# Latents' attention: projection in halves, two merge gates before its end, ten expert rows later

## The reference

```python
u = x * (1 + sc1) + sh1
xc, bg, cg, q, k, v, g_conv, g_na = jnp.split(u @ w_in, IN_SPLITS, axis=-1)
y_conv = short_conv(xc, bg, cg, conv_w)            # bg * conv3(cg * xc)
y_na = neighbourhood_attention(q, k, v, k_ctx, v_ctx, rpb)   # context tokens: plain attention
merged = (jax.nn.sigmoid(g_conv) * (y_conv @ w_conv_out) +
          jax.nn.sigmoid(g_na) * (y_na @ w_na_out))
x = layer_norm(ALPHA * x + ga1 * (merged @ w_o), ln1_g, ln1_b)
u2 = x * (1 + sc2) + sh2
x = layer_norm(ALPHA * x + ga2 * peer(u2, w_query, sub_keys, expert_u, expert_v), ln2_g, ln2_b)
```

## Time and profile before

| | us |
|---|---|
| median of 3 runs | 1879.93 (1879.83 to 1882.43) |
| the profiled execution | 1884.2 |
| its span, first to last instruction | 1882.4 |
| latents' attention on PE | 311.5 to 460.9 |
| latents' merge on PE | 460.9 to 630.3 |
| latents' norms, queries | 630 to 823 |
| stream of all experts | 823 to 1724 |

### The profile page before, as it was taken

How to read it: one execution, slowest core, us unless ns; L and a number is a source line. 1 busy time by engine, 2 the same in 40 slices (tenths; PEclk the granted TensorE clock), 3 DMA queues, 4 the chain that set the end, 5 groups by cost and what they waited for, 6 DMA issues and landing times.

```text
span 1882.4 us, 21570 instructions
## 1 busy us (share of the span) xinstructions
PE 1774.0 (94%) x8020; PEld 1143.8 (61%) x8020; DVE 1268.7 (67%) x2592; ACT 296.0 (16%) x665; POOL 894.2 (48%) x839
## 2 busy tenths in 40 slices
PE   5988999898999999998999999998889999999995
PEld 3675844454444359997888888886554434444442
DVE  1212568898589699988889768888865523236767
ACT  0120012554100011111100100106630000000000
POOL 1000336666455324253555645677865564435540
PEclk9998999999999999999999999999999999999998
DMA  9998779899999887589999999998999999999995
GB/s 395 396 344 314 266 206 391 307 333 324 365 364 389 346 291 284 179 320 372 363 407 393 391 347 407 409 406 322 353 349 409 409 409 409 409 409 409 409 410 227
DMA packets 171209, 670.22 MB, mean 356 GB/s; under 512 B 19771, under 2 KB 20923, under 8 KB 166365
## 3 DMA queue, kind: packets, MB, share of 16 engines
q0 software_dynamic: 112512, 410.26, 57.4%
q1 hardware_dynamic: 53840, 242.77, 33.0%
q10 hardware_dynamic: 4752, 15.81, 2.2%
HBM read 659.27 MB, written 7.39 MB: 354 GB/s over the span
## 4 chain that ended last, share of the span: by engine, by line
PE 65%; DVE 14%; DMA 10%; POOL 5%; issue 5%; ACT 1%; SPq 1%; ACTq 0%; DVEq 0%; POOLq 0%
PE psum L954 23%; PE psum L1028 16%; PE psum L1127 7%; DVE psum L1889 5%; POOL arena L612 5%; DMA arena<-in_expert_v_dram,arena 4%; PE psum L811 3%; DMA arena<-in_expert_u_dram,arena 3%; PE psum L786 2%; PE psum L1052 2%; PE psum L1055 2%; PE psum L981 2%; PE psum L1089 2%; PE psum L1115 1%; DMA arena<-in_w_ada_dram 1%
## 5 line engine op out<-in xcount | busy, mean ns | idle before, releaser
L612 POOL DMA_INDIRECT arena<-in_expert_u_dram,arena x384 | 468.5, 1220 | 354.1 <-DVE arena L1600 232.8
L1600 DVE CUSTOM_DVE_ANT_0 arena<-arena 128x1024 f32<-128x1024 f32 x384 | 459.5, 1222 | 167.3 <-DMA arena<-in_expert_u_dram,arena 154.5
L612 POOL DMA_INDIRECT arena<-in_expert_v_dram,arena x384 | 379.5, 988 | 360.2 <-DVE psum L1889 207.3
L1889 DVE SCALAR_TENSOR_TENSOR psum<-arena,psum 128x1024 f32<-128x1024 f32 x254 | 327.1, 1288 | 189.7 <-DMA arena<-in_expert_v_dram,arena 176.4
L954 PE MATMUL psum<-arena 128*128 128x256 f32 x2048 | 444.7, 380 | 6.6 <-DMA arena<-in_expert_uT_dram 6.6
L1028 PE MATMUL psum<-arena 128*128 128x512 f32 x1024 | 442.9, 594 | 0.4 <-DMA arena<-in_expert_v_dram 0.4
L954 PEld LDWEIGHTS psum<-arena 128*128 128x128 f32 x2048 | 390.6, 191 | 59.8 <-issue 7.0
L1028 PEld LDWEIGHTS psum<-arena 128*128 128x128 f32 x1024 | 193.7, 190 | 249.9 <-issue 249.6
L1127 PE MATMUL psum<-arena 128*128 128x128 f32 x1280 | 146.2, 275 | 1.4 <-DVE arena L1760 1.4
L1127 PEld LDWEIGHTS psum<-arena 128*128 128x128 f32 x1280 | 144.4, 192 | 3.3 <-issue 1.7
L1394 ACT ACTIVATE arena<-psum 128x512 f32<-128x512 f32 x64 | 38.2, 597 | 399.1 <-PE psum L954 399.1
(11 more groups left out here) (195 smaller groups left out, 1402.5 us busy)
## 6 DMA issues: line engine op xcount, KB each, us to landing
arena<-in_expert_uT_dram SPq DMA_DIRECT2D x128, 512.0 KB, 6.8
arena<-in_expert_v_dram SPq DMA_DIRECT2D x128, 512.0 KB, 6.8
arena<-in_w_ada_dram SPq DMA_DIRECT2D x12, 2048.0 KB, 16.5
arena<-in_w_in_dram SPq DMA_DIRECT2D x11, 2048.0 KB, 13.6
arena<-in_w_query_dram SPq DMA_DIRECT2D x8, 2048.0 KB, 12.7
arena<-in_w_in_dram SPq DMA_DIRECT2D x30, 512.0 KB, 7.4
arena<-in_w_o_dram SPq DMA_DIRECT2D x16, 512.0 KB, 5.3
arena<-in_expert_u_dram,arena POOLq DMA_INDIRECT x384, 8.9
```

The lines of the kernel that those rows point to most:

```text
L612: pool.indirect_dma_start(slot, None, table[0], bass.IndirectOffsetOnAxis(ap=number, axis=0)).then_inc(land, 16)
L1600: dve.tensor_tensor_reduce(UR[b], UR[b], U2B[e], 1.0, 0.0, ALU.mult, ALU.add, DOTS[e % 2][:, k:k + 1]).then_inc(u_free, 1)
L1889: dve.scalar_tensor_tensor(ys, row, weight, ys, ALU.mult, ALU.add).then_inc(v_free, 1)
```

## The change

It has five parts.

1. The pieces are cut into halves of 4 matmuls (`project_half`), and `HALVES` gives each pair from 0 to 13 one or two of them. A piece is opened by its first half (which waits for the copy of the piece ahead) and signalled by its second. Where a pair's two halves belong to two pieces (pairs 2, 3, 7 and 11) the second half there waits for ACT's copy of the piece that the first half has just ended; ACT's copy still stands at the end of its iteration (`PIECE_AFTER` now lists which pieces are copied in it).
2. The convolution gate of merge step 8 goes in two halves into pairs 14 and 15 (bank 5), that of step 9 stands whole between the last transposes and the last value product (bank 0). Merge steps 8 and 9 skip them; the sigmoid of step 8 becomes two instructions.
3. The convolutions move from behind the rows of pairs 2, 6, 10 to between the windows and the first row of pairs 3, 7, 11; the fourth stands behind the last pair.
4. Pair rows go from 70 to 60, the first two merge steps from 8 and 8 to 13 and 13.
5. The five parameter broadcasts move from the start of ACT's merge to behind its third sigmoid.

```diff
--- before.py
+++ after.py
@@ -113,8 +113,11 @@
 WHOLE, CONV_IN = (5, 3, 4), (0, 2, 1)
 PROJ_AT = tuple(range(6)) + tuple(6 + 4 * n for n in range(4))
 PROJ_CTX, PROJ_QKV = 6, PROJ_AT[-1]
-PIECE_AFTER = {0: 1, 1: 2, 2: 3, 4: 4, 5: 5, 6: 6, 8: 7, 9: 8, 10: 9, 12: 10, 13: 11}
-CONV_AFTER = {2: 0, 6: 1, 10: 2, 14: 3}
+HALVES = (2, 1, 2, 2, 1, 2, 1, 2, 1, 2, 1, 2, 1, 2)
+HALVES_TO = [2 + sum(HALVES[:i]) for i in range(len(HALVES) + 1)]
+PIECE_AFTER = {i: [m for m in range(1, 12) if HALVES_TO[i] <= 2 * m + 1 < HALVES_TO[i + 1]] for i in range(len(HALVES))}
+CONV_AFTER = {3: 0, 7: 1, 11: 2}
+GATE_HALVES, GATE_NEXT = {14: 0, 15: 1}, 16
 CONV_OPS = 5
 
 
@@ -801,15 +804,33 @@
                                            start=k == 0, stop=k == KD - 1)
                     mm.then_inc(proj_done, 1)
 
-            def project_piece(m):
-
+            def project_half(n):
+
+                m, half = divmod(n, 2)
                 c, i = divmod(m, len(CONV_IN))
-                weights(pe, ("conv", 1, c))
                 own = W_PARTS[slot_of["conv", 1, c]][:, i, :].rearrange("p (k n) -> p k n", n=P)
-                pe.wait_ge(proj_out, PROJ_QKV + m)
+                if half == 0:
+                    weights(pe, ("conv", 1, c))
+                    pe.wait_ge(proj_out, PROJ_QKV + m)
+                for k in range(4 * half, 4 * half + 4):
+                    mm = pe.matmul(bank(5), own[:, k, :], UT[:, k, CTX:NT], start=k == 0, stop=k == KD - 1)
+                if half == 1:
+                    mm.then_inc(proj_done, 1)
+
+            def first_gate(half):
+
+                wc = merge_weights(pe, "gconv", 1, 0, 0)
+                if half == 0:
+                    pe.wait_ge(proj_out, PROJ_QKV + 12)
+                for k in range(4 * half, 4 * half + 4):
+                    pe.matmul(bank(5), wc[:, k, :], UT[:, k, CTX:NT], start=k == 0, stop=k == KD - 1)
+
+            def second_gate():
+
+                wc = merge_weights(pe, "gconv", 1, 0, 1)
+                pe.wait_ge(win_step, NU - 2)
                 for k in range(KD):
-                    mm = pe.matmul(bank(5), own[:, k, :], UT[:, k, CTX:NT], start=k == 0, stop=k == KD - 1)
-                mm.then_inc(proj_done, 1)
+                    pe.matmul(bank(0), wc[:, k, :], UT[:, k, CTX:NT], start=k == 0, stop=k == KD - 1)
 
             pe.wait_ge(silu_step, 3)
             pe.wait_ge(cond_in, 48)
@@ -925,7 +946,8 @@
                 pe.wait_ge(po_out, 2)
 
             def latent_attention():
-                project_piece(0)
+                project_half(0)
+                project_half(1)
                 for i, n in enumerate(range(2, NU + 4, 2)):
                     if n < NU:
                         scores_of_pair(n)
@@ -934,8 +956,13 @@
                         turn(n - 1)
                     if n >= 6:
                         mix_of_pair(n - 4)
-                    if i in PIECE_AFTER:
-                        project_piece(PIECE_AFTER[i])
+                    if i < len(HALVES):
+                        for half in range(HALVES_TO[i], HALVES_TO[i + 1]):
+                            project_half(half)
+                    if i in GATE_HALVES:
+                        first_gate(GATE_HALVES[i])
+                    if i == GATE_NEXT:
+                        second_gate()
                 pe.wait_ge(po_out, outputs_upto(NU - 1))
 
             def expert_scores(m):
@@ -1047,9 +1074,10 @@
                         d = 8 * s + 4 * hf + c
                         if d >= 1:
                             pe.wait_ge(sig_out, d)
-                        wc = merge_weights(pe, "gconv", s, hf, c)
-                        for k in range(KD):
-                            pe.matmul(bank(0)[:, 0:n_tok], wc[:, k, :], UT[:, k, tok], start=k == 0, stop=k == KD - 1)
+                        if d not in (8, 9):
+                            wc = merge_weights(pe, "gconv", s, hf, c)
+                            for k in range(KD):
+                                pe.matmul(bank(0)[:, 0:n_tok], wc[:, k, :], UT[:, k, tok], start=k == 0, stop=k == KD - 1)
                         wn = merge_weights(pe, "gna", s, hf, c)
                         for k in range(KD):
                             mm = pe.matmul(bank(1)[:, 0:n_tok], wn[:, k, :], UT[:, k, tok], start=k == 0,
@@ -1290,8 +1318,8 @@
                         normalise(n + 1)
                     if n >= 6:
                         take_out(n - 3)
-                    if i in PIECE_AFTER:
-                        take_piece(PIECE_AFTER[i])
+                    for m in PIECE_AFTER.get(i, ()):
+                        take_piece(m)
 
             def normalise(n):
                 act.wait_ge(recip_done, n + 1)
@@ -1303,26 +1331,34 @@
 
             def load_x(e):
                 act.dma_start(XB[min(e, 1)], rows(x_prompt, x_sample, e)).then_inc(xb_in, 16)
+
+            def load_rows(s):
+
+                own = mods_d[s:s + 1, :]
+                for n, row in ((0, own[:, 2 * D:3 * D]), (1, ln1_g[0:1, :]), (2, ln1_b[0:1, :]),
+                               (3, own[:, 4 * D:5 * D]), (4, own[:, 3 * D:4 * D])):
+                    act.dma_start(PRM[s][n], row.partition_broadcast(P)).then_inc(prm_in[s], 16)
 
             def section(s):
                 t0, n_tok = SECTIONS[s]
                 if s == 0:
                     act.wait_ge(mods_out, 16)
-                else:
-                    act.wait_ge(win_step, NU - 2)
-                own = mods_d[s:s + 1, :]
-                for n, row in ((0, own[:, 2 * D:3 * D]), (1, ln1_g[0:1, :]), (2, ln1_b[0:1, :]),
-                               (3, own[:, 4 * D:5 * D]), (4, own[:, 3 * D:4 * D])):
-                    act.dma_start(PRM[s][n], row.partition_broadcast(P)).then_inc(prm_in[s], 16)
+                    load_rows(s)
                 for i in range(8):
                     d = 8 * s + i
                     act.wait_ge(gates_done, d + 1)
                     if d >= 1:
                         act.wait_ge(merge_step, 2 * d)
-                    src = bank(0, 2).rearrange("p (a b) -> p a b", a=2)[:, :, 0:n_tok]
-                    act.activation(SG[s], src, ACT.Sigmoid).then_inc(sig_out, 1)
+                    if d == 8:
+                        act.activation(SG[s][:, 0, :], bank(5), ACT.Sigmoid)
+                        act.activation(SG[s][:, 1, :], bank(1), ACT.Sigmoid).then_inc(sig_out, 1)
+                    else:
+                        src = bank(0, 2).rearrange("p (a b) -> p a b", a=2)[:, :, 0:n_tok]
+                        act.activation(SG[s], src, ACT.Sigmoid).then_inc(sig_out, 1)
                     if s == 1 and i == WEIGH_STEP:
                         weigh(0)
+                    if s == 1 and i == ROWS_STEP:
+                        load_rows(s)
                 if s == 0:
                     act.wait_ge(cache_out, 32)
                 load_x(s)
@@ -1615,13 +1651,14 @@
                     window(n)
                     window(n + 1)
                     rows = PAIR_ROWS[i]
+                    if i in CONV_AFTER:
+                        convolve_piece(CONV_AFTER[i])
                     context_rows(min(rows, 1))
                     normalise(n)
                     context_rows(min(rows - 1, 1))
                     normalise(n + 1)
-                    context_rows(rows - 2)
-                    if i in CONV_AFTER:
-                        convolve_piece(CONV_AFTER[i])
+                    context_rows(max(rows - 2, 0))
+                convolve_piece(3)
                 context_rows(BEFORE_MERGE)
 
             def route(e, part):
@@ -2046,9 +2083,10 @@
 PACE = NKEYS - RING - 9 - PACED_FROM
 assert (HK - BESIDE) % (2 * GROUP) == 0 and BESIDE % (2 * GROUP) == 0 and GATE_ROUNDS % 4 == 0
 FIRST_ROWS = 30
-PAIR_ROWS = (6, 6, 4, 2, 6, 6, 4, 2, 6, 6, 4, 2, 6, 6, 2, 2)
+PAIR_ROWS = (6, 3, 5, 3, 3, 6, 3, 3, 3, 6, 3, 3, 3, 6, 3, 1)
 BEFORE_MERGE = 12
-MERGE_ROWS, NORM_ROWS = (8, 8, 14, 14, 14, 14, 12, 3), 4
+MERGE_ROWS, NORM_ROWS = (13, 13, 14, 14, 14, 14, 12, 3), 4
+ROWS_STEP = 2
 WEIGH_STEP = 1
 CHOICE_ROWS = (5, 5, 5, 5, 4, 4, 4, 3, 3, 3)
 assert sum(MERGE_ROWS[:WEIGH_STEP + 1]) + BEFORE_MERGE + FIRST_ROWS + sum(PAIR_ROWS) == HK and len(CHOICE_ROWS) == 4 + PARTS
```

## The result

| | before | changed |
|---|---|---|
| median of 4 runs each | 1881.18 us | 1906.33 us |
| ratio, 95% interval | | 1.0133 (1.0107 to 1.0159) |
| span of the profiled execution | 1882.4 us | 1903.1 us |
| mean granted clock | 0.983 | 0.976 |

The change made the kernel 25 us slower; the interval of the ratio leaves out 1. I had forecast 10 slower, 1890.1 us, with a range up to 1901. The direction was right, the size was not. Ratios are of undisturbed executions only: one execution of the later kernel E7 took 6580.39 us and is left out, so E7 rests on three.

A forecast was written before the change was run, and what follows sets the result against it. TensorE was taken as the bound, with DVE setting the merge from step 10 on. Terms 6.6 + 1.4 - 1.0 + 3.2 gave +10.2 us, from a median of 1879.93 to 1890.1; range 1878 to 1901.

The forecast's parts named there:

- two signs of being wrong: Split waits under 1 us, or DVE entering merge step 10 before 523, would show the prediction wrong.
- A: Latents' attention up to the last transposes: +6.6 us, from about 0 to +10.
- C: First branch product to DVE's entry into merge step 10: 47.3 us, -1.0 against before.
- A, the old waits go: Latents' attention: TensorE's old waits vanish, -15.7 us, and the slow clock after the first long one, -2.7.
- A, pair 2: Pair 2 of the attention: +2.8 us waiting at the transposes, +1.4 at the split between two pieces.
- A, the split waits: Pairs 3, 7 and 11: second half waits 4.0 us for ACT's copy of the piece, three times, +12.0.
- A, the clock: Behind the three split waits: the clock falls after one in three, costing +1.7 us.
- B: Last transposes to first branch product: +1.4 us (-1.1 to +3.5), the branch weights' load replacing the gate taken out.
- D: Merge step 10 to output projection: +3.2 us, half of the five parameter broadcasts' 6.4 us of transfers.
- The rows in the attention are free: Latents' attention: the ten moved rows cost nothing there, since DVE would have had them hidden.
- the split is covered: Rival: pairs 2, 3, 7 and 11, copy done when the first half ends; A -8.5, sum -4.9, 1875 us; chance 0.10.
- Everything collides: Rival: three clock falls, late branch weights, slow rows, full broadcast cost: +10, +3.5, +4, +6.4, up to 1904; 0.13 above 1897.

The follow-up runs named there:

- E7: Changed kernel with ACT's piece copy ahead of the normalisations, ten rows back in the pairs and the second gate behind the last value product; 0.9910 of the kernel before.
- E1: Changed kernel, but in pairs 2, 3, 7 and 11 ACT copies value product and finished piece ahead of the two normalisations; 1.0040 of the kernel before.
- E3: Changed kernel with the ten rows back in the pairs (70 there, 8 and 8 in the first two merge steps); 1.0088 of the kernel before.
- E4: Changed kernel with the five parameter broadcasts back at the start of ACT's merge; 1.0118 of the kernel before.
- E6: Changed kernel with the second gate behind the last value product instead of ahead of it; 1.0069 of the kernel before.
- E9: Changed kernel, but POOL requests each gathered row of the first two tiles singly instead of in groups of four; 1.0104 of the kernel before.
- E12: E8 run once more, the same kernel; 0.9917 of the kernel before.
- E8: E7 with the five parameter broadcasts asked for at merge step 8 instead of step 10; 0.9896 of the kernel before.
- E2: Changed kernel, but in pairs 3, 7 and 11 DVE's convolution stands behind the pair's rows; 1.0032 of the kernel before.
- E11: Changed kernel with the halves undone, whole pieces where they stood before; 1.0109 of the kernel before.
- E10: E8 with four value rows moved from merge steps 10 to 13 to the normalisations behind the output projection; 0.9934 of the kernel before.

## Why the prediction was right and wrong, step by step

The mechanism was right in its parts: every wait that it named is in the trace, and neither of its two signs of being wrong appeared (the split waits are 3.97 us, DVE enters step 10 at 542.09). Two terms of the sum were sized wrongly, the clock in A and the rows in C, each with a clock price missing or too small.

- **What bounds the kernel**: right. TensorE is the chain up to step 10, and what is late there comes out at the end nearly one to one (E1: 16.7 us at the projection, 1.0133 to 1.0040, which is 17.5 us).
- **A, the old waits go**: right, -15.7 and -2.7 of clock. None of the waits of before is left.
- **A, pair 2**: 2.8 and 1.4 were forecast for transposes and split; measured are 1.28 + 0.55 and 0.78, and 1.6 of slow clock (0.4 on the transposes themselves, 1.2 on the products behind), which I had not listed. 4.2 forecast, 4.2 measured: that the sums agree is luck, with the waits put too high and a fall of the clock left out.
- **A, the split waits**: 4.0 us three times forecast, 3.97 measured, for the cause named.
- **A, the clock: the step that failed.** The prediction took one fall in three at 1.7 us, +1.7. It was three in three at 2.7 to 2.9, +8.3. Both factors were wrong. A wait of 4.0 lay between those of 1.2, which had left the clock alone (rows 4 don't show them; the row below does), and those of 4.76 and 5.05, and nothing in the trace of before told on which side. In the changed kernel and in E3, E4, E6 and E9 all 15 split waits, of 3.97 to 4.27 us, were followed by a fall. For the price I had used the average clock of a stretch behind the last transposes, where products are few. Here a half of a piece stood behind the wait, and its 3.67 us grew by three quarters. The same rows showed such a price, in the 2.7 us lost behind 346.72. The Trainium skill's rule, which the prediction quoted from TensorE: Matmul & The Clock Gate, "HAM oscillation — how this bites in real kernels", has the falls right: every round with such a wait was throttled anew. I gave that 0.05, and should have let it be the forecast.
- **B**: +2.2 for +1.4. Request at 10.5 us as worked out, landing 11.2 instead of 10.5. That a gate placed ahead of the last outputs gains nothing, because the load takes its place, was right, and E6 shows the place where it does gain.
- **C, the second step that failed**: 47.3 forecast, 54.7 measured. Of the 7.4, 2.7 are the clock behind the wait for the branch weights (the product took 6.26 instead of 3.60), which I had not charged although the wait was in my own sum. The other 4.7 are the rows: I had 37.5 us for 26 rows, of which 30.8 are 24 transfers at 409 GB/s and some 3 the way to the first request; for the remaining 3.7 the prediction gives no source. The 30.8 take the queues to be full from the first request on. From 500.83 to 515 they moved 261 GB/s instead, while the first requests came 2.29 us apart. At 409 GB/s what was not moved in these 14.17 us is worth 5.1 us, an estimate from these two rates. That the slow requests are the whole reason is argued and not shown.
- **D**: +1.3 for +3.2. Once DVE enters step 10 on time it is +4.4 (E3), and with the broadcasts in step 8 it is 1.7 to 3.2 less than with them in step 10 (E7 against E12 and E8). That the late entry hid the term in the changed kernel is my reading. C and D were not independent, which the sum took them to be: C falls by 10.4 in E3 and D grows by 3.1, in E6 by 2.3 and 2.1.
- **The rows in the attention are free**: right for E7's order (A 129.3 with 70 rows, E1 130.5 with 60). In the changed kernel's order they add 2.1 us of waits (E3), which A doesn't show because the clock happened to stay up in pair 2.
- **The rivals**: "the split is covered" would have come true with the copy ahead of the normalisations (E1) or the convolution behind the rows (E2). "Everything collides" up to 1904 was nearest; of its four parts the clock was dearer than it had it (8.3 for 5.1), and the clock behind the branch weights was missing. It had B (3.5 for 2.2) and D (6.4 for 1.3) too dear, so that it came near is partly luck.
- **The range**: its upper end stood on 1.7 us as the price of a fall. With the measured price of a fall alone, three instead of one at 1.7, A would have been +13.2 and the sum +16.8, 1897.

About 0.9 us of A has no term: old waits and clock, gate, pair 2, split waits and their clock sum to 13.1 of 14.0. In E1 the same 0.9 us is over. Most of it is probably the price of a half: an undisturbed half takes 3.70 us as one run, a whole piece 7.13, and the first transposes to the last hold twenty halves.

The row on the clock, from the trace of before: a wait of 1.24 us, and four records behind it that take 0.66, where the four behind the wait of 4.76 took 1.22 (0.70 undisturbed):

```profile
385.97 0.66 PE L878 MATMUL psum<-arena 128*128 128x128 f32 x4 [1.24 <-ACT arena L1298]
```

E8 is the better kernel: the halves, the gates in the attention and the convolutions' place stay; ACT's copy stands ahead of the normalisations, the ten rows are back in the pairs, the second gate stands behind the last product and the parameters are asked for at step 8. It is 0.8 to 1.0% faster than before.

## What to carry to other kernels

A unit of work cut in two needs its hand-over cut free as well: look where the copy that frees the bank stands in the other engine's order, and what that engine waits for ahead of it. A wait of TensorE of about 4 us was to be charged twice here, once for itself and once for the slow work behind it: 2.7 to 2.9 us with a half of a piece behind it, 2.1 with transposes and value products (E11: 2.32 and 1.98 us instead of 1.10 and 1.09). And a ring that was full and has to refill behind a fast consumer does not get the bandwidth of a saturated stretch at once: here it was 261 GB/s over the first 14 us, and 410 then.

## What was not expected of the hardware

**Gather requests slow down while DVE reduces rows.** In the changed kernel an indirect request of POOL takes 0.94 us when DVE rests, and 1.99 when the row reductions follow each other without a pause. The page's groups show it over the whole program (busy us, mean ns of one):

```profile
L615 POOL DMA_INDIRECT arena<-in_expert_u_dram,arena x384 | 456.0, 1188 | 408.1 <-DVE arena L1636 283.4
...
L615 POOL DMA_INDIRECT arena<-in_expert_v_dram,arena x384 | 378.0, 984 | 345.1 <-DVE psum L1926 209.5
```

The first are requested mostly beside row reductions (L1636, both inputs and the output in SBUF), the second beside L1926, which reads and writes PSUM. Of the requests of the whole program, 131 had at least 0.85 of their first 0.94 us beside row reductions, and 82 of them (63%) took over 1.2 us; of 128 that stood so beside L1926 none did, nor did any of the 109 beside which DVE did nothing. It is not the table: three of six requests for `expert_v` beside row reductions were slow too. So a faster consumer can slow its own supply. Why a third of the requests beside row reductions were not slowed is open. The Trainium skill's page SBUF — State Buffer, section "Who interferes with whom", has VectorE and GpSimd share one port pair as an exclusive lock; of VectorE's two-port modes it says that who issues first holds the pair for the whole instruction and the other is blocked. The extra 1.05 us, near the 1.15 us of a row, agree with such a lock. The same section lets a VectorE operation with two inputs in SBUF stand in the way of GpSimd's reads alone; which access of the request is held up here, no run shows.

**Equal waits, unequal clock.** In pair 2 the waits of 1.1 to 1.5 us at the transposes were followed by a fall of the granted clock in the changed kernel, E1, E2, E4 and E9, and by none in E3, E6, E7, E8, E10 and E12; in the changed kernel it cost 1.6 us, in E2 about 2.9. E3's wait of 2.29 us in pair 2 was followed by none either. The split waits of 0.78 in pairs 3, 7 and 11 were never followed by one, those of 3.97 us and more always. This fall is in A of some kernels and not of others, with the same instructions there, so differences in A of 1 to 2 us are not to be put down to an edit.
